# A hybrid decoder step with a 32-expert mixture: router logits in column tiles, biases and gathers in other places, TensorE fed from the first microsecond

## The reference

```
h = rmsnorm(x, norm1_g);  z = h @ w_in                       # 1024 x 2824
y1 = s5_mixer(...);  y2 = rglru_mixer(...);  y3 = mlstm_mixer(...)
x = x + concat(y1, y2, y3) @ w_out
# mixture of experts on rmsnorm(x, norm2_g)
logits = xf @ router_w + router_b                            # 288 x 32
top_val, top_idx = top_k(logits, 4);  gates = softmax(top_val)
for each expert e, for the rows that chose it:
    hb = row @ w1[e] + b1[e];  g = min(hb[:D_FF], 7);  u = clip(hb[D_FF:], -7, 7)
    out += gate * ((g * sigmoid(1.702 g) * (u + 1)) @ w2[e] + b2[e])
return rmsnorm(x + out, final_norm_g), new states
```

## Time and profile before

| | before |
|---|---|
| median of 3 runs | 1125.26 us (1124.24 to 1125.68) |
| the profiled execution: time | 1126.33 us |
| its span, first to last instruction | 1124.5 us |
| TensorE matmul busy | 1049.7 us (93%) |
| VectorE, ScalarE, GpSimd busy | 323.7, 188.6, 96.9 us |
| read from HBM | 425.19 MB, 381 GB/s over the span |
| mean granted TensorE clock | 0.988 |

### The profile page before, as it was taken

How to read it: one execution, slowest core, us unless ns; L and a number is a source line. 1 busy time by engine, 2 the same in 40 slices (tenths; PEclk the granted TensorE clock), 3 DMA queues, 4 the chain that set the end, 5 groups by cost and what they waited for, 6 DMA issues and landing times.

```text
span 1124.5 us, 13162 instructions
## 1 busy us (share of the span) xinstructions
PE 1049.7 (93%) x5142; PEld 444.2 (40%) x5142; DVE 323.7 (29%) x642; ACT 188.6 (17%) x379; POOL 96.9 (9%) x179
## 2 busy tenths in 40 slices
PE   7999999999999999899889998999899989998996
PEld 5666755433433342333233423242334333433332
DVE  5789554421212111212121212121212120202023
ACT  5433613520101020102010100010001000100002
POOL 6886300000000000000000000000000000000000
PEclk9999999899999999999999999999999999999998
DMA  7430689999999999999999999999999999999995
GB/s 233 170 110 26 206 313 344 372 393 430 425 431 432 429 430 431 434 431 431 431 433 431 431 430 433 431 431 430 434 430 431 431 433 430 431 430 431 425 427 209
DMA packets 57379, 429.96 MB, mean 382 GB/s; under 512 B 9910, under 2 KB 20894, under 8 KB 30078
## 3 DMA queue, kind: packets, MB, share of 16 engines
q1 hardware_dynamic: 56196, 428.68, 91.3%
q10 hardware_dynamic: 1146, 0.79, 0.2%
HBM read 425.19 MB, written 3.67 MB: 381 GB/s over the span
## 4 chain that ended last, share of the span: by engine, by line
PE 59%; DMA 36%; DVE 1%; SPq 1%; issue 1%; ACT 1%; DVEq 0%; PEldq 0%
DMA ring_a<-in_exp_w_dram 23%; PE psum L2331 18%; PE psum L2357 12%; DMA ring_b<-in_exp_w_dram 11%; PE psum L2343 7%; PE psum L1801 5%; PE psum L2257 3%; PE psum L2280 3%; PE psum L1813 3%; DMA acts<-in_router_b_dram 2%; PE psum L2366 1%; PE psum L2211 1%; PE psum L2217 1%; PE psum L2112 1%; SPq L428 1%
## 5 line engine op out<-in xcount | busy, mean ns | idle before, releaser
L2331 PE MATMUL psum<-ring_a,xg 128*64 128x512 f32 x1184 | 345.4, 600 | 14.0 <-DMA ring_a<-in_exp_w_dram 14.0
L2357 PE MATMUL psum<-ring_a,aT 128*64 128x512 f32 x768 | 221.1, 596 | 9.7 <-DMA ring_a<-in_exp_w_dram 9.4
L2331 PEld LDWEIGHTS psum<-ring_a,xg 128*64 128x64 f32 x1184 | 103.8, 137 | 167.9 <-issue 164.1
L2331 PE MATMUL psum<-ring_b,xg 128*64 128x512 f32 x368 | 159.6, 598 | 8.3 <-DMA ring_a<-in_exp_w_dram 8.3
L1625 DVE TENSOR_TENSOR x<-x,psum 128x512 f32<-128x512 f32 x64 | 44.0, 688 | 384.6 <-PE psum L2280 384.6
L2343 PE MATMUL psum<-ring_a,xg 128*64 128x512 f32 x352 | 107.7, 608 | 16.1 <-DMA ring_b<-in_exp_w_dram 16.1
L2357 PEld LDWEIGHTS psum<-ring_a,aT 128*64 128x64 f32 x768 | 69.2, 137 | 113.4 <-issue 108.1
L2357 PE MATMUL psum<-ring_b,aT 128*64 128x512 f32 x256 | 107.7, 596 | 4.6 <-DMA ring_a<-in_exp_w_dram 2.7
L1694 DVE TENSOR_SCALAR acts<-psum 128x512 f32<-128x512 f32 x32 | 22.0, 688 | 224.8 <-PE psum L2343 209.5
L2331 PEld LDWEIGHTS psum<-ring_b,xg 128*64 128x64 f32 x368 | 45.0, 136 | 75.8 <-issue 63.5
L1001 ACT ACTIVATE acts<-acts 128x512 f32<-128x512 f32 x32 | 20.0, 625 | 299.8 <-DVE acts L1694 299.8
(11 more groups left out here) (485 smaller groups left out, 951.2 us busy)
## 6 DMA issues: line engine op xcount, KB each, us to landing
ring_a<-in_exp_w_dram SPq DMA_DIRECT2D x144, 2048.0 KB, 26.4
ring_b<-in_exp_w_dram SPq DMA_DIRECT2D x46, 2048.0 KB, 24.8
ring_a<-in_w_in_dram SPq DMA_DIRECT2D x5, 2048.0 KB, 7.5
ring_a<-in_w_out_dram SPq DMA_DIRECT2D x2, 2048.0 KB, 9.7
ring_a<-in_state_ml_c_dram SPq DMA_DIRECT2D x4, 512.0 KB, 6.1
out_dram<-ring_a SPq DMA_DIRECT2D x4, 512.0 KB, 9.5
ring_b<-in_exp_w_dram SPq DMA_DIRECT2D x2, 1024.0 KB, 29.3
xn<-in_x_prompt_dram SPq DMA_DIRECT2D x2, 512.0 KB, 4.2
```

Of the source, the lines that this page charges most:

```text
L2331: m = M(psum[64 * x:64 * x + 64, bk, :], xg[:, k, u, 64 * x:64 * x + 64], cols, start=False, stop=(k == KD - 1))
L2357: m = M(psum[64 * x:64 * x + 64, 4 + nn, :], aT[:, 2 * j + s, 64 * x:64 * x + 64], w[x][:, 1024 * s + 512 * nn:1024 * s + 512 * nn + 512], ...
```

## The change

- **Opening.** A tile `warm` (512 bf16 columns of 1.0) is set as VectorE's first instruction. TensorE multiplies it into the unused bank 7: 14 times ahead of everything, once after the first two `turn_half`, once after the fourth, twice after the last (`keep_warm`). Chunk 0 of w_in is loaded in two DMAs of 256 columns, and the right one is awaited only ahead of xr0.
- **Logits of tiles 0 and 2.** The router columns are stationary, 32 at a time in four column tiles, and the rows move: 16 matmuls give four partial sums (fill "parts", bank 7). ScalarE copies them out, behind `mean_square(1, 2)`. Two matmuls against `part_adds` (a new VectorE reduction ahead of the memsets) add them, after k = 2 of `output(1, 1, k)`. Tile 1 is as before.
- **Order behind that.** Biases of banks 2, 0 and 3 go ahead of the last mask; three matmuls without a reader (bank 5) stand in front of "cum1"; of "cum1" only its last matmul is left behind the mask; the gathers of chunk 2 (tiles 0, 2) follow it, and those of tile 1 for chunks 0 and 1 go ahead of chunk 3.
- **Counts.** The three matmuls for the totals are gone. The maximum is taken over the running count (after S is made), whose row 127 has the totals; `cnt` is read from partition 127.

Core of the diff:

```diff
-_place(["wo00", "wo01"], (6, 7))
+_place(["wo00", "wo01", "parts"], (6, 7, 7))
...
+                if c == 0:
+                    for x in range(2):
+                        sp.dma_start(slot_view(0, 512)[:, :, 256 * x:256 * x + 256], w_in_cols(WCH[0][0] + 256 * x, 256)).then_inc(
+                            sem(("w_in0", "w_in0_right")[x]), 16)
...
             mean_square(1, 2)
+            copy_out("parts", logit_parts, bank("parts")[:, 0:128 + TS])
...
+            V.memset(warm, 1.0).then_inc(sem("warm_ready"), 1)
...
+            V.tensor_reduce(part_adds, ident[:].rearrange("p (j c) -> p c j", j=4), AX.X, ALU.add).then_inc(sem("part_adds_ready"), 1)
...
-            drains(V.tensor_reduce(st2[:, 8:9], bank("cum1")[:, NE:2 * NE], AX.X, ALU.max), "cum1")
             dve.wait_ge(*at("rows_scaled", 1))
             TT(S[:, :, 1], spread(slot[:, 0:2, 1, :].unsqueeze(3), 3, SLOTS), slots_of_two(), ALU.is_equal).then_inc(sem("s_ready"), 1)
+            drains(V.tensor_reduce(st2[:, 8:9], bank("cum1")[:, 0:NE], AX.X, ALU.max), "cum1")
...
+            def keep_warm(n):
+
+                for _ in range(n):
+                    M(psum[:, 7, :], warm[:, 0:128], warm, start=True, stop=True)
+
+            pe.wait_ge(sem("warm_ready"), 1)
+            keep_warm(14)
...
+            def partial_logits():
+
+                await_bank(pe, "parts")
+                for i, c0_ in ((0, 0), (2, 128)):
+                    t0, n = TILES[i]
+                    for k in range(KD):
+                        if k % 4 == 0:
+                            b, f = FILLS[f"h2T{2 * i + k // 4}"]
+                            pe.wait_ge(drained[b], f + 1)
+                        j = 32 * (k % 4)
+                        m = M(bank("parts")[j:j + 32, c0_:c0_ + n], rw[:, k, :], h2T[:, k, t0:t0 + n], start=(k < 4), stop=(k >= 4))
+                ends_fill(m, "parts")
...
+                for i, c0_ in ((0, 0), (2, 128)):
+                    n = TILES[i][1]
+                    m = M(bank("lg")[0:n, NE * i:NE * i + NE], logit_parts[:, c0_:c0_ + n], part_adds, start=True, stop=True)
+                ends_fill(m, "lg")
```

More of the change, by code:

```diff
@@ L210, in build_program @@
         nst = ms("nst", [128, 16])
+        warm = gsm[:, 0, 0:256].bitcast(BF16)
         uT_rolled = ms("uT_rolled", [128, 2, T])
@@ L1782, in _ @@
             turn_half(1)
+            keep_warm(1)
             pe.wait_ge(sem("vec_loaded"), 16 * 11)
@@ L2170, in turn_rows, with logits, added_logits @@
                     ends_fill(m, name)
[L2172 to L2175, removed]
+            def logits(hf):
+                t0, n = TILES[1]
+                b, f = FILLS[f"h2T{2 + hf}"]
                 pe.wait_ge(drained[b], f + 1)
                 for k in range(4 * hf, 4 * hf + 4):
-                    m = M(out, h2T[:, k, t0:t0 + n], rw[:, k, :], start=(k == 0), stop=(k == KD - 1))
+                    m = M(bank("lg1")[:, 0:NE], h2T[:, k, t0:t0 + n], rw[:, k, :], start=(k == 0), stop=(k == KD - 1))
                 return m
+            def partial_logits():
[9 more added lines that the diff above has]
+                ends_fill(m, "parts")
+            def added_logits():
+                await_bank(pe, "lg")
+                pe.wait_ge(sem("part_adds_ready"), 1)
+                b, f = FILLS["parts"]
+                pe.wait_ge(drained[b], f + 1)
+                for i, c0_ in ((0, 0), (2, 128)):
+                    n = TILES[i][1]
+                    m = M(bank("lg")[0:n, NE * i:NE * i + NE], logit_parts[:, c0_:c0_ + n], part_adds, start=True, stop=True)
+                ends_fill(m, "lg")
             for k in range(KD):
@@ L2191, in _ @@
                     pe.wait_ge(sem("router_loaded"), 48)
[L2192 to L2196, removed]
+                    partial_logits()
+                if k == 2:
+                    added_logits()
                 if k == 6:
@@ L2225, in _ @@
             await_bank(pe, "lg1")
-            logits(1, 0)
-            ends_fill(logits(1, 1), "lg1")
+            logits(0)
+            pe.wait_ge(sem("selb_ready"), 1)
+            bias(2, 1024)
+            ends_fill(logits(1), "lg1")
+            bias(0, 0)
             gather_first(1, (0, 2))
-            gather_first(2, (0, 2))
-            pe.wait_ge(*at("mask_ready", 2))
             await_bank(pe, "cum1")
@@ L2234, in _ @@
             M(cum[:, 0:NE], ones_bf[0:TS, :], mskb[0:TS, 2, :], start=False, stop=False)
[L2235 to L2238, removed]
-            gather_first(3, (0, 2))
[L2240 to L2245, removed]
+            b, f = FILLS["lg1"]
+            pe.wait_ge(drained[b], f + 1)
+            bias(3, 1536)
+            for _ in range(3):
+                M(psum[:, 5, 0:256], ones_bf[0:96, :], bsplit[0:96, 0:256], start=True, stop=True)
+            pe.wait_ge(*at("mask_ready", 2))
+            ends_fill(M(cum[:, 0:NE], upper[:], mskb[:, 1, :], start=False, stop=True), "cum1")
+            gather_first(2, (0, 2))
+            pe.wait_ge(sem("s_ready"), 1)
+            gather_first(0, (1,))
+            gather_first(1, (1,))
+            gather_first(3, (0, 2))
+            gather_first(2, (1,))
+            gather_first(3, (1,))
             b, f = FILLS["cum1"]
```

17 lines of the change are left out of this document (12 added, 5 removed).

## The result

| | before | changed |
|---|---|---|
| median of 5 runs each | 1125.27 us (1124.24 to 1127.77) | 1118.73 us (1118.58 to 1119.35) |
| ratio of the medians, 95% interval | | 0.994 (0.9928 to 0.9953) |
| the profiled execution: time | 1126.33 us | 1119.35 us |
| its span | 1124.5 us | 1117.6 us |
| TensorE matmul busy | 1049.7 us | 1049.6 us |

The changed kernel is 6.5 us faster in the median and 6.9 us in the span of the profiled executions. TensorE is busy for as long as before: the 18 added matmuls stand where it was idle, and what was gained elsewhere stands against them.

A forecast was written before the change was run, and what follows sets the result against it. The prediction saw one DMA weight stream whose early holes hang on TensorE. Gains of 2.3 us at the start and 3.5 in the routing sum to 5.8, giving 1119.5 us as a median (chance 0.45), range 1117.8 to 1124.0.

The forecast's parts named there:

- What bounds the kernel: Whole kernel: the DMA weight stream is full from 240 us; its earlier holes wait on TensorE at 145.9 and 206.5 us.
- My sum of its holes: DMA stream at 205 to 215 and 235 to 240 us: missing shares add to 2 us, or 4.1 us by GB/s.
- The start, 2.3 us: First 32 channel instructions: fillers keep TensorE from starting slow, 8.16 us instead of 10.45, saving 2.3 us (bounds 0 and 2.3).
- routing only: Rival: the opening stays slow because transposes leave TensorE thin, only the routing's 3.5 us is gained; 1121.8 us, chance 0.18.
- The fourteen fillers: Ahead of the first transposes: take 3.4 to 6.5 us, end between 4.7 and 7.8 us, at worst 1 us late.
- GpSimd's margin: S5 scans, GpSimd's third turn: its 3.10 us wait exceeds the 2.3 us gained at the opening, 0.8 left over.
- The logits, 0.7 us: Logits of tiles 0 and 2: column tiles 1.0 us plus 0.4 for the sum replace 2.33; 0.7 us earlier from there.
- Behind the second mask: From the second mask to expert step 0: the new order, with the mask at 197.5, starts step 0 3.5 us earlier.
- I take the clock as held: Routing after 199 us: full clock assumed, where half clock had cost 2.6 us; otherwise step 0 only 1.3 us earlier.
- start only: Rival: the opening's 2.3 us is gained but the clock still falls in the routing, leaving 1.3 there; 1121.7 us, chance 0.17.
- The low end of the range: Forecast less 1.7 us, if 16 gathers take 0.2 us each instead of 0.30: 1117.8 us.
- slower: Rival: column-tile logits leave TensorE thinner, clock falls before 185 us and stays down through the outputs; 1128 us, chance 0.06.

The follow-up runs named there:

- the second set of runs: The changed kernel measured once more with nothing altered: median 1119.64 us over 6 runs, ratio 0.9956 to the kernel before.
- two sets of runs (1122.84 and 1121.06): Changed kernel with the earlier order behind tile 1's logits, new logits kept and readerless matmuls out, measured twice: 1122.84 us (8 runs) and 1121.06 us (12 runs).

## Why the prediction was right, and where its steps were not

The forecast was 1119.5 us, 5.8 less than before; it came out at 1118.73 (and 1119.64 in the second set of runs). The likeliest case was the one that came, in its main features. Step by step:

- **What bounds the kernel.** Right, and better borne out than I could know. Two constant stretches (122.1 and 34.2 us) show that a gain at the start reaches the routing whole, and the rest behind step 0 stays between 917.5 and 920.2 us however early step 0 comes (918.5, 917.8 and 918.9 at the three earliest). The queue takes nothing that shows. My sum of its holes left out 230 to 235 us (0.85, 311 GB/s), with which it is 5.5 us by GB/s and not 4.1; the 7.32 us at step 0 lose 0.4 in the rest, within what that stretch varies by (before itself 918.1 and 919.1).
- **The start, 2.3 us.** Measured: 2.87 in the pair of traces (2.45 by rate, 0.32 by an earlier hT, 0.1 behind), but 1.2 as a mean over traces. The mechanism is right. The step that failed is "the engine is then never left empty": 1.10 to 1.34 us are empty, and in four of seven traces the clock fell behind them, those in which the fourteen had been slowest. My rival "routing only" had the right reason, but as a case of its own and not as what happens in about half of the executions. The Trainium skill (TensorE: Matmul & The Clock Gate, Part 1) says that the number of slow matmuls at the start differs from run to run; here 8.00 and 9.69 us for the same program agree.
- **The fourteen fillers** end at 6.68 us, inside 4.7 to 7.8, and delay no transpose (6.76, before 6.81). The half load of w_in cost nothing visible.
- **GpSimd's margin.** Right, with 1.28 us left over and not 0.8. The third turn waits that long for VectorE, in the timeline of GpSimd in the changed kernel, in place of 3.10:

```profile
83.30 1.41 POOL L690 TENSOR_TENSOR xn<-ring_a,tabc 128x576 f32<-128x576 f32 x1 [1.28 <-DVE ring_a L1397]
```

- **The logits, 0.7 us.** Mis-sized: 1.1 at the new order (22.95 - 21.85) and 1.1 at the old one (22.84 - 21.72). The block took 0.70 and not 1.0, the sum of the parts 0.32 and not 0.4. I had placed the copy at 184.3 us and the first mask at 189.0, 0.9 later. In the changed kernel all of this runs 2.9 us earlier, and counted from the turned rows the mask is only 0.6 later, since the copy follows the parts directly (180.75 us). No drain shows around the column tiles: output, 32 narrow instructions and output follow each other without a wait in the chain.
- **Behind the second mask.** The sum of both routing terms was 3.5 and came to 4.46 (26.31 - 21.85). It divides differently from my working: logits 1.1, counts 0.26, order -0.1 (21.72 - 21.85), clock 3.2 (26.31 - 23.10). I had 0.7 for the logits, about 0.6 for order and counts, and 2.2 for the clock. The largest term, the clock, came in because the fall is frequent in the kernel before and rarer in the changed one, as far as their runs tell, and not because the order decides it. That the two profiled executions showed it whole, and the start whole too, is in part luck. The gathers at 0.27 in place of 0.30 are in it.
- **"I take the clock as held."** It held in the changed kernel's traces, but the reason I gave was too strong. The clock can hold with the old order (three of five traces) and fall with the new one (one of nine). What I read as a property of a place in the order is a chance that the order shifts. The rival "start only" at 1121.7 was priced by one certain fall; in no trace of the changed kernel does it come. The one of its eleven runs that took as long (1122.42) has a mean clock of 0.992, which speaks against a fall there too.
- **The three readerless matmuls.** I counted them as part of the filling. No run shows a benefit.
- **The low end of the range.** Sixteen gathers at 0.2 in place of 0.30 are 1.6 us, not 1.7; nothing hangs on it. They came at 0.27.

The rival "slower" wanted a fall before 185 us; none of the fourteen traces shows one between 180 and 185 us.

The 6.9 us between the two spans are, by stretch: 2.9 at the start, 4.46 in the routing, less 0.4 in the rest and 0.1 of rounding. Of the routing 3.2 are the fall of the clock in this execution of before, and 1.25 what is left with the clock held in both (23.10 - 21.85): 1.1 the logits, 0.26 the counts, -0.1 the order. Of the start about 1.2 is what the fillers give as a mean over traces. So the size of the gain in the medians rests in good part on how often the clock falls in either kernel, which one trace each could not show. No version tried beats the changed kernel by more than its runs scatter.

## What to carry to other kernels

Cut the span at events that stay a constant distance apart over several traces; then each edit is read from its own stretch to a tenth of a microsecond, where the median of one program differed by 1.8 us between two sets of runs (1122.84 and 1121.06). Trace the same program twice before you tie a fall of the clock to an edit: it came and went in one program, at the start and in the routing, and cost 1.7 to 4 us. And if TensorE is to be fed, feed it right up to the first real work: with a microsecond left empty, four of seven executions lost 1.5 of the 2.1 us that the feeding had bought (the first 32 end at 22.7 us as a mean, not 21.2, against 23.3 unfed), and with the gap closed or nearly so, neither of two did. Half of the fillers, at either end, gave nothing.

## What was not expected of the hardware

- A granted clock that falls to 0.50 while TensorE is busy all the time: in the kernel with more fillers and no readerless matmuls it held up to about 194 us and then stayed at 0.50 for 10 us, through 512- and 256-column matmuls without a gap between them. What went ahead was busy 3.00 of 3 us too (190 to 193 us, narrow logits and biases).
- 32 float32 instructions of 128 and 32 columns in four column tiles took 0.70 us, 0.022 each; the 32 that made the same logits with stationary rows and 32 moving columns took 2.33.
- The same fourteen fillers took 5.14, 5.69, 4.87 and 6.15 us in four traces: how soon TensorE comes to its full rate differs from execution to execution. In the seven traces of one opening this came with what happened 7 us later: 5.22 us or less and the clock held at u0, 5.38 or more and it fell.
